# Start bytes of TensorE's operands in a decoder block: equal modulo 512 in output projection and MLP, eight other distances in the input projection

## The chip, the cores and the metric

One core of a Trainium2 chip runs the whole block in one launch. The metric is the device time in microseconds (us) of that launch; smaller is better.

## The reference

One decoder block on `x` of 2048 rows and 1024 columns, all in float32:

```python
h = rmsnorm(x, g_pre_mix)
proj = einsum('bsd,dc->bsc', h, w_in)             # 1024 x 3080
fox  = forgetting_attention(fq, fk, fv, f_logit)  # 8 heads of 64
diff = differential_attention(dq, dk, dv, ...)    # 4 heads of 2 x 64, values of 128
mix = einsum('bsc,cd->bsd', concatenate([fox, diff]), w_out)
x = x + rmsnorm(mix, g_post_mix)
h = rmsnorm(x, g_pre_mlp)
u = square(relu(einsum('bsd,df->bsf', h, w_up)))  # 1024 x 4096
x = x + rmsnorm(einsum('bsf,fd->bsd', u, w_down), g_post_mlp)
```

Both attentions are causal and take a softmax over the keys.

## The kernel before

The kernel keeps float32 accuracy by splitting each operand of a large product into a high and a low part (`_hi`, `_lo`) and running three matmuls for each: hi x hi, hi x lo and lo x hi. Nearly all of them are 128 x 128 stationary by 128 x 512 moving. In `nc.matmul(out, stationary, moving)` the second argument is loaded into the array by an instruction of its own (PEld in the profile) while the matmul before it is still streaming its moving operand; a profile's row names them the other way round, `out<-moving,stationary` (in the rows of L673 to L675 `pj_acc<-pj_v_hi,pj_h_early` has v_hi moving).

There are four stages, each with an order of work written out by hand for every engine.

- **Input projection** (`project`): the 16 tiles of normalised rows are turned and split into `keep.h_early` (rows 0 to 1023) and `h_late` (rows 1024 to 2047). For the q and k columns the weights `w_hi`, `w_lo` are stationary and h moves (L665 to L667); for the v columns h is stationary and `v_hi`, `v_lo` move (L673 to L675).
- **Attention** (`attend`): scores `ps_s` from `k1`, `k2` moving and `q1`, `q2` stationary (L1376, L1382), transposes of `probs` (L1400), and products with `v_sb` stationary and `p_hi`, `p_lo` moving (L1415 to L1420). A planner with costs and due times sets the order.
- **Output projection** (`mix_out`): for each of 16 tiles of rows `m_hi`, `m_lo` are stationary, `w_hi` and `w_lo` move (L1648 to L1650; for the last two of eight steps of k the low part is `keep.w_lo_end`, otherwise `w_lo_begin`), 48 matmuls, then 8 transposes (L1658) of the tile before.
- **MLP** (`mlp`): two halves of 1024 rows; in each, 16 chunks of 256 hidden columns. A chunk's first product (`up`, L2011 to L2014) has `up_hi`, `up_lo` stationary and `h2_rows_hi`, `h2_rows_lo` moving, 96 matmuls; its second product (`down`, L2032 to L2036) has `u_hi`, `u_lo` stationary and `dn_hi`, `dn_lo` moving, 96 matmuls in 16 groups of six, each added into `y` by VectorE (L1976). In the last chunk of a half VectorE normalises finished tiles (L1963) and GpSimd adds the residual (L1851).

All tiles in SBUF are taken from one pointer that runs upwards, through `Room.sb` (L41); each starts at the next multiple of 32 bytes. The rows of all these operands, and the steps between the slices that a matmul takes, are multiples of 512 bytes, so the start of a tile modulo 512 is the start of every slice of it. Worked out from the order of allocation:

| tiles | start, bytes modulo 512 | address range, bytes |
|---|---|---|
| `h_early`; `q1`, `q2`, `k1`, `k2`, `p_hi`, `p_lo`; `m_hi`, `m_lo`, `w_lo_end`; `u_hi`, `u_lo`; `ident_r` | 128 | below 98,944 |
| `h_late`, projection's `w_hi`, `w_lo`, `v_hi`, `v_lo` | 64 | 100,416 and up |
| `v_sb`, `probs`; `rows_hi`, `rows_lo`; output projection's `w_hi`, `w_lo_begin`; `up_hi`, `up_lo`, `dn_hi`, `dn_lo` | 320 | 99,648 and up |

Of the kernel before, what the change touches and what calls it, by code (L numbers as in the profile page):

```python
# [12 lines left out]
P = 128  # L13
# [16 lines left out]
def f32(ap):  # L30

    return ap.bitcast(F32)


class Room:
# [4 lines left out]

    def sb(self, name, shape, dt=F32):  # L41
        return self.ctx.enter_context(self.nc.sbuf_tensor(f"{self.stage}_{name}", shape, dt))

    def ps(self, name, shape):
        return self.ctx.enter_context(self.nc.psum_tensor(f"{self.stage}_{name}", shape, F32))
# [155 lines left out]
def project(nc, keep, x, g_pre_mix, w_in, b_forget, lams, g_subln, qk, vals, q_rows, k_rows):  # L201
# [36 lines left out]
    with ExitStack() as ctx:  # L238
        r = Room(nc, ctx, "pj")
# [3 lines left out]
        rstd = r.sb("rstd", [P, RT])  # L243
        power = r.sb("power", [P, 1])
        eps = r.sb("eps", [P, 1])
        h_late = r.sb("h_late", [P, 2, KT, S // 2], F32R)
        raw = r.sb("raw", [P, 2, KT, P])
        w_hi = r.sb("w_hi", [P, 2, KT, P], F32R)
        w_lo = r.sb("w_lo", [P, 2, KT, P], F32R)
        lam_in = r.sb("lam_in", [P, 4, HD])  # L250
        acc = r.ps("acc", [P, 8, 512])
        with ExitStack() as early:
            e_room = Room(nc, early, "pje")
            xin = e_room.sb("xin", [P, XR, D])
            xn = e_room.sb("xn", [P, 2, D])
            gain = e_room.sb("gain", [P, D])
            junk = e_room.sb("junk", [P, D], mybir.dt.bfloat16)
            wl_raw = e_room.sb("wl_raw", [P, KT, H])
            wl = e_room.sb("wl", [P, KT, 2 * H], F32R)
            b = e_room.sb("b", [P, 1])  # L260
            z, z2, az, e, w, lw, t1, c = (e_room.sb(name, [P, SEG])
                                          for name in ("z", "z2", "az", "e", "w", "lw", "t1", "c"))
            c_hi, c_lo = (e_room.sb(name, [P, SEG], F32R) for name in ("c_hi", "c_lo"))
            carry = e_room.sb("carry", [P, 1])
            ones, negs, zeros, tri = (e_room.sb(name, [P, SEG]) for name in ("ones", "negs", "zeros", "tri"))
            pos = e_room.sb("pos", [SEGS, SEG])
            up = e_room.sb("up", [SEGS, D4, SEG])
        v_hi = r.sb("v_hi", [P, KT, 512], F32R)
        v_lo = r.sb("v_lo", [P, KT, 512], F32R)

        x_loaded = [r.sem(f"x_loaded{s}") for s in range(XR)]
# [701 lines left out]
def attend(nc, keep, qk, vals, q_rows, k_rows, mixT, w_out, x):  # L973
# [44 lines left out]
    with ExitStack() as ctx:  # L1018
        r = Room(nc, ctx, "at")
        k1, k2, q1, q2, p_hi, p_lo = keep.k1, keep.k2, keep.q1, keep.q2, keep.p_hi, keep.p_lo  # L1020
        k_loaded, q_loaded = keep.k_loaded, keep.q_loaded
        ident_r, nlam, gsub = keep.ident_r, keep.nlam, keep.gsub
        ident = f32(ident_r[:, :])
        o_sb = r.sb("o_sb", [P, ORING, 512])
        v_sb = r.sb("v_sb", [P, 6, 4, 256], F32R)
        probs = r.sb("probs", [P, PROB_COLUMNS])
# [1016 lines left out]
def hybrid_block(nc, x, g_pre_mix, w_in, b_forget, lambda_q1, lambda_k1, lambda_q2, lambda_k2,  # L2043
                 g_subln, w_out, g_post_mix, g_pre_mlp, w_up, w_down, g_post_mlp, out):
    qk = nc.dram_tensor("qk", [16, 2, P, S], F32).ap()
    vals = nc.dram_tensor("vals", [2, 4, S, 256], F32).ap()
    q_rows = nc.dram_tensor("q_rows", [4, FOX_HEADS + DIFF_HEADS, S], F32).ap()
    k_rows = nc.dram_tensor("k_rows", [4, FOX_HEADS + DIFF_HEADS, S], F32).ap()
    mixT = nc.dram_tensor("mixT", [KT, P, S], F32).ap()
    x2 = nc.dram_tensor("x2", [S, D], F32).ap()  # L2050
    h2T = nc.dram_tensor("h2T", [2, KT, P, S // 2], F32).ap()
    with ExitStack() as ctx:
        keep = Lasting(nc, ctx)
        project(nc, keep, x, g_pre_mix, w_in, b_forget, (lambda_q1, lambda_k1, lambda_q2, lambda_k2), g_subln,
                qk, vals, q_rows, k_rows)
        attend(nc, keep, qk, vals, q_rows, k_rows, mixT, w_out, x)
        r = Room(nc, ctx, "h2")
        rows_hi = r.sb("rows_hi", [P, KT, S // 2], F32R)
        rows_lo = r.sb("rows_lo", [P, KT, S // 2], F32R)
        mix_out(nc, keep, mixT, x, g_post_mix, g_pre_mlp, x2, h2T, rows_hi, rows_lo, w_up)  # L2060
        mlp(nc, keep, rows_hi, rows_lo, h2T, w_up, w_down, x2, g_post_mlp, out)
# [22 lines left out]
```

How the kernel before makes its waits and increments, by code:

```python
    def wait_mixed(self, eng):  # L162
        for s in range(ORING):
            eng.wait_ge(self.o_stored[s], 16 * ((4 * 8 + ORING - 1 - s) // ORING))
# [170 lines left out]
        @block.sync  # L336
# [1 line left out]
            def load_x(t):  # L338
                if t >= XR:
                    sp.wait_ge(xn_ready, t - XR + 1)
                sp.dma_start(xin[:, t % XR, :], x[0, bass.ts(t, P), :]).then_inc(x_loaded[t % XR], 16)
# [1 line left out]
            def load_piece(z):  # L343
                what, n, _ = pieces[z]
                col = column_of(what, n)
                if z >= 2:
                    sp.wait_ge(w_ready, z - 1)
                sp.dma_start(raw[:, z % 2], w_v[:, :, col:col + P]).then_inc(raw_loaded[z % 2], 16)
# [6 lines left out]
            load_x(3)  # L355
            load_piece(0)
            load_x(4)
            load_piece(1)
            for t in range(5, RT):
                load_x(t)
            load_piece(2)
            load_piece(3)
            for job in jobs:
                if job.what == "logit":
                    sp.wait_ge(stored[job.out % OR], 16 * (job.out // OR + 1))
            for n, dst in enumerate((z, z2)):
                sp.dma_start(dst[:, :], logits[n].rearrange("h (s j) -> (h s) j", j=SEG)).then_inc(z_loaded, 16)
            for n, v in enumerate(lams):
# [4 lines left out]
            for job in jobs:  # L373
                if job.what == "qk" and job.n in (0, 4):
                    sp.wait_ge(stored[job.out % OR], 16 * (job.out // OR + 1))
            sp.wait_ge(rows_stored, ROWS)
```

## Time and profile before

| | us |
|---|---|
| median of 3 runs | 3103.01 |
| lowest and highest run | 3100.74, 3103.22 |
| the profiled execution | 3099.3 |
| its span, first to last instruction | 3096.9 |
| TensorE busy in it (matmuls) | 2952.1 |
| VectorE, ScalarE, GpSimd busy | 1678.8, 1022.6, 1005.6 |

The span falls into the projection (to about 583 us), attention (to 1424), the output projection (to 1636) and the MLP. A matmul's recorded duration runs on after the next one has started, so the sum of the durations of a line is not the time that it takes; the starts of consecutive matmuls give that. TensorE's clock has two levels, 1.2 and 2.4 GHz; in the profile's granted clock 1.00 is the higher.

### The profile page before, as it was taken

The page shows a single profiled execution, that of the slowest core. Times are in us where ns is not written, and L with a number is a line of the kernel's source. Part 1 is how long each engine was busy: PE and PEld are TensorE (multiplying, and loading weights), DVE is VectorE, ACT ScalarE, POOL GpSimd, SP SyncE. Part 2 cuts the span into 40 slices and gives each one's busy share as a digit, 9 for nine tenths or more (in the row PEclk, how much of TensorE's full clock was granted, in tenths as well). Part 3 has the DMA queues.
Part 4 walks back from the last instruction along what each step waited for, and adds up shares of the span by engine and source line. Part 5 has one row for each costly group of instructions (what it writes and reads, how often), then busy time and mean ns, then how long its engine had stood idle before and what let it go on. Part 6 is the DMA issues. An engine that isn't in the chain of part 4 may idle for free. (4 is left out here: it accounts for less than half of the span.)

```text
span 3096.9 us, 39329 instructions
## 1 busy us (share of the span) xinstructions
PE 2952.1 (95%) x14082; PEld 2411.1 (78%) x14082; DVE 1678.8 (54%) x2505; ACT 1022.6 (33%) x1973; POOL 1005.6 (32%) x733
## 2 busy tenths in 40 slices
PE   7999999998998989988998999999999999999996
PEld 5888888777877778877876888888887788888885
DVE  5211111389898898996554444444446544444446
ACT  4121111387786877863221111111112111111111
POOL 4220020157466465571113222222225222222224
PEclk9999999999999999999998999999999999999998
DMA  5342342833434144323732011101134110111022
GB/s 171 124 143 102 111 139 94 204 77 85 103 95 111 52 118 118 78 78 117 223 122 75 28 54 54 54 27 54 54 135 164 55 54 27 54 54 54 28 75 88
DMA packets 205240, 282.78 MB, mean 91 GB/s; under 512 B 12032, under 2 KB 135168, under 8 KB 205120
## 3 DMA queue, kind: packets, MB, share of 16 engines
q1 hardware_dynamic: 150976, 213.19, 23.7%
q10 hardware_dynamic: 53376, 67.25, 6.1%
q8 instruction: 70, 1.15, 0.2%
q0 software_dynamic: 768, 0.79, 0.1%
q14 instruction: 50, 0.41, 0.1%
HBM read 196.38 MB, written 84.80 MB: 91 GB/s over the span
## 5 line engine op out<-in xcount | busy, mean ns | idle before, releaser
L1976 DVE TENSOR_TENSOR ml_y<-ml_y,ml_ps_y 128x512 f32<-128x512 f32 x512 | 351.3, 686 | 246.9 <-PE ml_ps_y L2036 242.0
L2032 PE MATMUL ml_ps_y<-ml_dn_hi,ml_u_hi 128*128 128x512 f32 x1024 | 408.6, 399 | 10.5 <-DVE ml_y L1976 10.5
L2011 PE MATMUL ml_ps_u<-h_rows_hi,ml_up_hi 128*128 128x512 f32 x1024 | 400.7, 391 | 9.5 <-POOL ml_up_lo L1829 9.5
L2036 PE MATMUL ml_ps_y<-ml_dn_hi,ml_u_lo 128*128 128x512 f32 x1024 | 406.1, 397 | 0.0
L2034 PE MATMUL ml_ps_y<-ml_dn_lo,ml_u_hi 128*128 128x512 f32 x1024 | 406.1, 397 | 0.0
L2013 PE MATMUL ml_ps_u<-h_rows_lo,ml_up_hi 128*128 128x512 f32 x1024 | 400.3, 391 | 0.0
L2014 PE MATMUL ml_ps_u<-h_rows_hi,ml_up_lo 128*128 128x512 f32 x1024 | 400.1, 391 | 0.0
L1278 DVE TENSOR_REDUCE at_nmax<-at_ps_s 128x1 f32<-128x1024 f32 (+7 forms) x384 | 347.0, 907 | 47.8 <-PE at_ps_s L1382 43.4
L1952 DVE TENSOR_TENSOR ml_relu<-ml_relu 128x512 f32<-128x512 f32 x128 | 94.6, 739 | 492.0 <-ACT ml_relu L1915 492.0
L1836 POOL TENSOR_TENSOR ml_dn_lo<-ml_dn_raw,ml_dn_hi 128x1024 fp32r<-128x1024 f32 x64 | 155.6, 2454 | 546.1 <-ACT ml_dn_hi L1905 546.1
L1829 POOL TENSOR_TENSOR ml_up_lo<-ml_up_raw,ml_up_hi 128x1024 fp32r<-128x1024 f32 x64 | 168.4, 2653 | 500.0 <-ACT ml_up_hi L1895 500.0
L588 DVE SCALAR_TENSOR_TENSOR pj_out_sb<-pj_acc,pj_out_sb 128x512 fp32r<-128x512 f32 x96 | 66.4, 692 | 429.2 <-ACT pj_out_sb L524 429.2
L1287 DVE TENSOR_TENSOR at_p_lo<-at_ps_t,at_p_hi 128x512 fp32r<-128x512 f32 x480 | 280.4, 602 | 27.2 <-ACT at_p_hi L1249 25.5
L1400 PE MATMUL at_ps_t<-at_ident_r,at_probs 128*128 128x128 f32 x1632 | 250.9, 278 | 37.0 <-DVE at_p_lo L1287 32.4
L1249 ACT ACTIVATE at_p_hi<-at_ps_t 128x512 fp32r<-128x512 f32 x480 | 248.9, 532 | 92.9 <-PE at_ps_t L1400 59.2
L1905 ACT ACTIVATE ml_dn_hi<-ml_dn_raw 128x1024 fp32r<-128x1024 f32 x64 | 64.6, 1054 | 629.8 <-PE ml_ps_y L2036 606.7
L1240 ACT ACTIVATE at_probs<-at_ps_s,at_nmax 128x1024 f32<-128x1024 f32 (+7 forms) x256 | 237.6, 929 | 91.5 <-DVE at_nmax L1278 83.1
L1400 PEld LDWEIGHTS at_ps_t<-at_ident_r,at_probs 128*128 128x128 f32 x1632 | 196.5, 143 | 82.6 <-issue 33.5
L1915 ACT ACTIVATE ml_relu<-ml_ps_u 128x512 f32<-128x512 f32 x128 | 76.5, 599 | 554.2 <-PE ml_ps_u L2014 528.8
L2032 PEld LDWEIGHTS ml_ps_y<-ml_dn_hi,ml_u_hi 128*128 128x128 f32 x1024 | 193.1, 189 | 63.6 <-DVE ml_y L1976 18.5
L2011 PEld LDWEIGHTS ml_ps_u<-h_rows_hi,ml_up_hi 128*128 128x128 f32 x1024 | 193.4, 189 | 50.9 <-issue 10.3
L1376 PE MATMUL at_ps_s<-at_k,at_q 128*128 128x512 f32 (+3 forms) x640 | 213.8, 399 | 17.3 <-ACT at_probs L1240 14.2
(229 smaller groups left out, 5707.5 us busy)
## 6 DMA issues: line engine op xcount, KB each, us to landing
qk<-pj_out_sb ACTq DMA_DIRECT2D x64, 512.0 KB, 2.8
ml_up_raw<-in_w_up_dram SPq DMA_DIRECT2D x32, 1024.0 KB, 5.6
ml_dn_raw<-in_w_down_dram SPq DMA_DIRECT2D x32, 1024.0 KB, 7.6
at_q<-qk SPq DMA_DIRECT2D x96, 256.0 KB
at_k<-qk SPq DMA_DIRECT2D x96, 256.0 KB
vals<-pj_out_sb ACTq DMA_DIRECT2D x32, 512.0 KB, 2.9
at_v_sb<-vals SPq DMA_DIRECT2D x32, 512.0 KB, 3.9
pj_raw<-in_w_in_dram SPq DMA_DIRECT2D x24, 512.0 KB, 4.0
```

The source lines that it names most:

```text
L1240: act.activation(out, ps_s[:, sc.g % 2, 0:sc.width], ACT.Exp, bias=bias, accum_out=rsum[:, par, sc.a, s, sc.part:sc.part + 1]).then_inc(ex ...
L1249: act.activation(p_hi[:, t.n % PRING, t.off:512], ps_t[:, at % TRING, t.off:512], ACT.Copy)\
L1278: dve.tensor_reduce(nmax[:, par, sc.a, s, sc.part:sc.part + 1], ps_s[:, sc.g % 2, 0:sc.width], AX.X, ALU.max, negate=True).then_inc(maxed, 1)
L1287: dve.tensor_tensor(p_lo[:, t.n % PRING, t.off:512], ps_t[:, at % TRING, t.off:512], f32(p_hi[:, t.n % PRING, t.off:512]), ALU.subtract).t ...
L1400: last = pe.transpose(ps_t[:, at % TRING, a * P:(a + 1) * P], probs[:, key:key + P], ident)
L1976: dve.tensor_tensor(y[:, t, cols], y[:, t, cols], ps_y[:, b % 4, :], ALU.add)\
L2011: pe.matmul(ps_u[:, b % 4, :], up_hi[:, k, cols], h_hi[:, k, rows], start=(k == 0), stop=False)
L2013: pe.matmul(ps_u[:, b % 4, :], up_hi[:, k, cols], h_lo[:, k, rows], start=False, stop=False)
L2014: last = pe.matmul(ps_u[:, b % 4, :], up_lo[:, k, cols], h_hi[:, k, rows], start=False, stop=(k == KT - 1))
L2032: pe.matmul(ps_y[:, b % 4, :], u_hi[:, s, f, rows], dn_hi[:, f, cols], start=(f == 0), stop=False)
L2034: pe.matmul(ps_y[:, b % 4, :], u_hi[:, s, f, rows], dn_lo[:, f, cols], start=False, stop=False)
L2036: last = pe.matmul(ps_y[:, b % 4, :], u_lo[:, s, f, rows], dn_hi[:, f, cols], start=False, stop=(f == FT - 1))
```

## The change

A new method of `Room` places a tile without use, a gap, so that the next tile starts at a given byte modulo 512:

```diff
+    def start_at(self, offset):
+        base = -(-self.nc.sbuf_base // 32) * 32
+        if (offset - base) % 512:
+            self.sb(f"gap{base}", [P, (offset - base) % 512 // 4])
...
         eps = r.sb("eps", [P, 1])
+        r.start_at(96)
         h_late = r.sb("h_late", [P, 2, KT, S // 2], F32R)
         raw = r.sb("raw", [P, 2, KT, P])
+        r.start_at(128)
         w_hi = r.sb("w_hi", [P, 2, KT, P], F32R)
+        r.start_at(160)
         w_lo = r.sb("w_lo", [P, 2, KT, P], F32R)
...
+        r.start_at(224)
         v_hi = r.sb("v_hi", [P, KT, 512], F32R)
+        r.start_at(352)
         v_lo = r.sb("v_lo", [P, KT, 512], F32R)
...
         ident = f32(ident_r[:, :])
+        r.start_at(128)
         o_sb = r.sb("o_sb", [P, ORING, 512])
...
         r = Room(nc, ctx, "h2")
+        r.start_at(128)
         rows_hi = r.sb("rows_hi", [P, KT, S // 2], F32R)
```

No engine has an instruction more or less, or in another place; only addresses in SBUF change, and the line numbers (by 6 to 13). The tiles that follow a gap move with it:

| stage | tiles | before | after |
|---|---|---|---|
| projection | `h_early` | 128 | 128 |
| | `h_late` | 64 | 96 |
| | `w_hi`, `w_lo` | 64, 64 | 128, 160 |
| | `v_hi`, `v_lo` | 64, 64 | 224, 352 |
| attention | `v_sb`, `probs` | 320 | 128 |
| | `q1`, `q2`, `k1`, `k2`, `p_hi`, `p_lo` | 128 | 128 |
| output projection | `m_hi`, `m_lo`, `w_lo_end` | 128 | 128 |
| | `w_hi`, `w_lo_begin` | 320 | 128 |
| MLP | `rows_hi`, `rows_lo`, `up_hi`, `up_lo`, `dn_hi`, `dn_lo` | 320 | 128 |
| | `u_hi`, `u_lo` | 128 | 128 |

## Rows read from the trace of the kernel before

**Rows 1.** Stretches by stage: from:to, length, PE busy (count), PEld, DVE, ACT, POOL, clock

```profile
90.00:583.00 493.00, 493.00 (x2155) 404.24 (x2154) 66.45 (x108) 74.82 (x114) 62.02 (x28) 1.00 0.37 123
583.00:1424.00 841.00, 768.80 (x4548) 639.39 (x4546) 740.94 (x1340) 631.61 (x1428) 487.00 (x370) 0.98 0.39 97
1424.00:1636.00 212.00, 195.97 (x896) 159.35 (x896) 114.86 (x102) 58.13 (x88) 25.87 (x66) 0.96 0.53 159
1636.00:3097.00 1461.00, 1424.93 (x6144) 1157.05 (x6144) 709.16 (x914) 217.86 (x286) 387.31 (x190) 0.99 0.18 63
```

**Rows 2.** TensorE's waits over the span, longest: us in total, times, longest

```profile
PE at_ps_t L1400 <- DVE at_p_lo L1287: 32.4, 24, 5.6
```

**Rows 3.** TensorE in order of time, MLP: start us, us; first product, then second

```profile
1987.30 0.39 PE L2011 MATMUL ml_ps_u<-h_rows_hi,ml_up_hi 128*128 128x512 f32 x1
...
1995.24 0.39 PE L2014 MATMUL ml_ps_u<-h_rows_hi,ml_up_lo 128*128 128x512 f32 x1
...
2003.21 0.39 PE L2032 MATMUL ml_ps_y<-ml_dn_hi,ml_u_hi 128*128 128x512 f32 x1
...
2016.97 0.40 PE L2036 MATMUL ml_ps_y<-ml_dn_hi,ml_u_lo 128*128 128x512 f32 x1
```

**Rows 4.** Groups by line and shape, MLP: count, busy us, mean ns of one, idle

```profile
L2034 PE MATMUL ml_ps_y<-ml_dn_lo,ml_u_hi 128*128 128x512 f32 x1024 | 406.1, 397 | 0.0
...
L2013 PE MATMUL ml_ps_u<-h_rows_lo,ml_up_hi 128*128 128x512 f32 x1024 | 400.3, 391 | 0.0
```

**Rows 5.** The same view, projection

```profile
L665 PE MATMUL pj_acc<-pj_h_early,pj_w_hi 128*128 128x512 f32 x256 | 101.7, 397 | 0.0
L667 PE MATMUL pj_acc<-pj_h_early,pj_w_lo 128*128 128x512 f32 x256 | 100.5, 392 | 0.0
L665 PE MATMUL pj_acc<-pj_h_late,pj_w_hi 128*128 128x512 f32 x256 | 100.4, 392 | 0.0
L667 PE MATMUL pj_acc<-pj_h_late,pj_w_lo 128*128 128x512 f32 x256 | 99.9, 390 | 0.0
L666 PE MATMUL pj_acc<-pj_h_late,pj_w_hi 128*128 128x512 f32 x256 | 99.6, 389 | 0.0
L666 PE MATMUL pj_acc<-pj_h_early,pj_w_hi 128*128 128x512 f32 x256 | 99.6, 389 | 0.0
...
L673 PE MATMUL pj_acc<-pj_v_hi,pj_h_early 128*128 128x512 f32 x128 | 50.6, 396 | 0.0
...
L673 PE MATMUL pj_acc<-pj_v_hi,pj_h_late 128*128 128x512 f32 x128 | 49.8, 389 | 0.0
```

**Rows 6.** The same view, output projection: whole span, then 1466.13 to 1466.15 us

```profile
L1649 PE MATMUL mo_acc<-mo_w_lo_begin,mo_m_hi 128*128 128x512 f32 x180 | 71.1, 395 | 0.0
...
L1649 PE MATMUL mo_acc<-mo_w_lo_end,mo_m_hi 128*128 128x512 f32 x1 | 0.4, 388 | 0.0
```

**Rows 7.** The same view, attention: whole span, then 1109.00 to 1109.69 us

```profile
L1416 PE MATMUL at_ps_o<-at_p_lo,at_v_sb 128*128 128x512 f32 x224 | 88.2, 394 | 0.0
...
L1376 PE MATMUL at_ps_s<-at_k,at_q 128*128 128x512 f32 x2 | 0.6, 389 | 0.0
```

**Rows 8.** VectorE and TensorE in order of time, output projection: start us, us

```profile
1505.76 1.28 DVE L1591 SCALAR_TENSOR_TENSOR mo_xn<-mo_y,mo_rstd,mo_g_pre 128x1024 f32<-128x1024 f32 x1
...
1507.67 1.23 DVE L1578 TENSOR_TENSOR mo_m_lo<-mo_m_raw,mo_m_hi 128x1024 fp32r<-128x1024 f32 x1
...
1509.09 1.04 PE L1658 MATMUL mo_flip<-at_ident_r,mo_xn 128*128 128x128 f32 x8
1509.88 0.48 PE L1648 MATMUL mo_acc<-mo_w_hi,mo_m_hi 128*128 128x512 f32 x1
```

**Rows 9.** The chain that ended last, its end: start us, us, what

```profile
3061.87 0.24 PE ml_ps_y L2036
...
3064.17 2.41 POOL ml_xres L1851
...
3092.61 1.23 DVE ml_xres L1987
```

## The prediction

> **What bounds the kernel now.** Read the stretches first [rows 1]: TensorE is busy 493.0 of 493 us in the projection, 196 of 212 in the output projection and 1424.9 of 1461 in the MLP. Only attention leaves a real gap (768.8 of 841), and its longest wait in total is 32.4 us on VectorE [rows 2]. In three of four stages the time is therefore a count of matmuls times the distance from one start to the next. No instruction moves here, so the question is that distance, for matmuls with 512 columns.
>
> A matmul's recorded duration does not give it directly, since consecutive ones overlap. The starts do. In the MLP's first product 35 matmuls start between 1987.30 and 1995.24 us, 226.9 ns each; in its second product 59 start between 2003.21 and 2016.97, 233.2 ns each [rows 3]. (Starts are printed to 10 ns; I use 226.7 and 233.3.) The recorded durations over all 1024 of a line are 391 and 397 [rows 4]: about the spacing plus 162 to 164 ns, so differences between recorded means can be read as differences of spacing.
>
> Both products have the same shape, the same engine and the same weight load before each matmul. What differs in the table of bytes: in the first product the stationary tile (up_hi, up_lo) and the moving tile (rows_hi, rows_lo) both stand at 320 modulo 512; in the second the stationary tile (u) is at 128 and the moving one (dn) at 320. The projection has the same pair side by side. With the same v_hi and the same line, h_early (128 against 64) takes 396 and h_late (64 against 64) 389; with w_hi at 64, h_early's three lines take 397, 389 and 392, h_late's 392, 389 and 390 [rows 5]. So equal bytes give the cheap mark of 389, unlike ones mostly 392 to 397. While a matmul streams its moving operand, the next one's stationary operand is loaded (a PEld instruction beside each matmul), so I read this as the two reads meeting in SBUF, and the distance that counts as moving tile minus the stationary tile loaded meanwhile.
>
> **The change, part by part.**
>
> *MLP, second product.* All of u, dn_hi and dn_lo stand at 128, so distance 192 becomes 0. There are 32 passes of 96 matmuls. Thirty of them run on TensorE's path in full: 30 x 96 x 6.6 ns = 19.0 us. The last pass of each half hands over early: after its fifth group of six the chain goes to VectorE and then to GpSimd, which alone takes it from 3064 to the end at 3093 [rows 9]; only some 30 matmuls of each count, 0.4 us. Nothing takes the gain away: the next product waits for no other engine (TensorE busy throughout), and VectorE, which adds up every six matmuls, is busy 709 of 1461 us [rows 1]. Term: **-19.4 us**, bounds -18 (after a break a stream may need some matmuls until its spacing is regular) and -20.5.
>
> *MLP, first product.* From 320/320 to 128/128, distance 0 both times. Is 128 as good as 320? Two rows say yes: in the output projection w_lo_end (128) streams while m_lo (128) is loaded, and there the recorded time is 388 where w_lo_begin (320) has 395 over all [rows 6]; in attention a run of scores, keys and queries all at 128, shows 389 [rows 7]. Term: **0**.
>
> *Output projection.* m_hi, m_lo stay at 128, w_hi and w_lo_begin go from 320 to 128: distance 192 becomes 0. After each block of transposes the first matmul waits for its weights and keeps its time; 15 tiles x 47 x 6.6 ns = 4.7 us, less a little for settling. It must also reach the end: the normalised tile is ready at 1507.04 for transposes at 1509.09, and the split of the next input at 1508.90 for a product at 1509.88 [rows 8]. Slack 2.0 and 1.0 us, and the period shrinks by 0.3. Term: **-4.2 us**, bounds -3.5 and -4.7.
>
> *Attention.* v and probs move to 128, so the products with v go from distance -192 to 0; scores were at 0. At most 784 full-width matmuls (two lines of 224, three of 112) x (394 - 389) = 3.9 us [rows 7]. But scores already have equal bytes and their runs are two to six matmuls between transposes, too short to settle. And this stage waits on other engines too. Term: **-0.5 us**, bounds -3.9 and +0.5 (no row shows equal bytes slower than unlike ones, so the loss is bounded by that alone).
>
> *Projection.* Here bytes that agree are pulled apart. Distances (moving minus stationary): h_early/w_hi 0 (was 64), h_early/w_lo -32 (64), h_late/w_hi -32 (0), h_late/w_lo -64 (0), v_hi/h_early 96 (-64), v_hi/h_late 128 (0), v_lo/h_early 224 (-64), v_lo/h_late 256 (0). Before, the spacing sums to 768 x 231.0 + 768 x 228.5 + 384 x 233.2 + 384 x 226.8 ns = 529.5 us (each mean is the busy time of its lines in [rows 5] over their count, less 162 ns; the two v groups by one line of three). Of the new distances the trace shows 0 (226.7) and, for v, -64 (233.3). Bounds from rows: all at 226.7 gives 522.3 us, -7.2; all at the 397 of h_early's dearest line, 235, gives +11.9. I take 233.3 for every distance but 0, the value that both 192 and -64 have and hence the nearest: h_late with w 768 x 233.3 (+3.7), v with h_late 384 x 233.3 (+2.5), v with h_early unchanged (0), and h_early with w, where two of three loads are at 0, 228.9 (-1.6). Term: **+4.7 us**. TensorE is busy without a break, so all of it counts.
>
> **Sum.** -19.4 - 4.2 - 0.5 + 4.7 = -19.4 us. The profiled execution took 3099.3 us (span 3096.9 and 2.4 around it), so 3079.9 for it; the runs' median is 3103.0, 3.7 higher, so **3083.6**. With the bounds of MLP, output projection and attention, and the projection between 0 and +8.1 (all at 233.3): 3077 to 3092.
>
> **The rivals.**
>
> *The projection's new distances are cheap.* If all are near 226.7, its term is -7 and the time 3072 (3068 to 3077). For: distance 64 is not uniformly dear, one of h_early's lines has 389. Against: -64, one of the new distances, is in the trace and dear.
>
> *They are dearer than anything seen.* At 235 the term is 12 and the time 3091; with starts at odd multiples of 32 (96, 160, 224, 352), which no operand of these matmuls has now, up to 3097. Nothing shows such a step; nothing excludes it.
>
> *It doesn't do what it says: the tile's place matters, not its byte.* Before the change all tiles at 128 lie below address 98,944 and all at 64 or 320 above it, so "both tiles in the same part of the memory" sorts every row as well as "both at the same byte": u and dn, h_early and v_hi, m and w_lo_begin are pairs across that border and dear, h_late and w, rows and up above it, w_lo_end and m_lo below it cheap [rows 3 to 6]. By place, moving tiles up by 32 to 320 bytes changes nothing: 3103. Against it: two reads that get in each other's way should do so within one part, not across two.
> The Trainium skill's rule would also end here: "TensorE: Matmul & The Clock Gate", Step-by-step: what each phase is for, says that TensorE has two independent SBUF read ports and that loading the next weights takes no bandwidth from the running matmul; by it no start byte could change the spacing, and the sum would be 0. The trace does not agree that the spacing is free of where the operands lie: 396 against 389 with one line and one v_hi [rows 5].
>
> *Slower: what is fast is the byte 64 modulo 256, not equality.* Every long cheap stretch now has both operands at 64 or 320, every dear one an operand at 128. Then MLP and output projection, all at 128, are dear: the second product gains nothing and the first loses 32 x 96 x 6.6 ns = 20.3 us; with +4.7 in the projection 3128. It decides in the first product: slower as soon as its recorded mean rises from 391 by over 5 ns with none gained in the second. Against it stand the 388 and 389 at 128 [rows 6, 7], short stretches both.
>
> **How the numbers follow.** Forecast 0.63, cheap projection 0.15, dear projection 0.09, nothing changes 0.09, slower 0.04. The likeliest case gives 3083.6. The range 3070 to 3094 takes the forecast, most of the cheap case and half of the dear one: 0.8. A measurement of this kernel can tell about 0.2% from no change, 6.2 us, so faster means below 3096.8: 0.63 + 0.15 + 0.08 = 0.86; same 0.10 (place, and what is left of the dear case); slower 0.04.
>
> **What would show it.** Right: L2013 and L2034 of before, by their new line numbers, both at a recorded 389 to 392; the output projection's lines at 389 to 391 apart from the first after transposes; h_late's lines near 395, v's near 395. The forecast falls if the MLP's first product leaves 391, or if the second stays at 397. If both hold and the time is off, the projection's rows say by how much each distance differs from 233.3.

## Result and profile after

The changed kernel takes 3087.44 us (median of 4 runs, 3082.47 to 3087.71); the kernel before, run beside it, 3101.88 us. The ratio is 0.9949, with a 95% interval of 0.9935 to 0.9964: 14.4 us faster. The profiled execution of the changed kernel took 3087.21 us, its span 3085.1.

First the stretches by stage (columns as in [rows 1]; each stretch begins and ends at about the first matmul of a stage):

```profile
90.00:592.00 502.00, 499.76 (x2159) 404.43 (x2157) 67.17 (x109) 75.44 (x115) 61.93 (x28) 1.00 0.37 122
592.00:1431.00 839.00, 769.32 (x4544) 640.62 (x4544) 740.89 (x1340) 631.69 (x1428) 487.68 (x370) 0.97 0.39 97
1431.00:1638.00 207.00, 191.84 (x896) 159.58 (x896) 114.26 (x101) 57.52 (x87) 25.55 (x66) 0.96 0.54 162
1638.00:3085.00 1447.00, 1408.08 (x6144) 1156.47 (x6144) 707.74 (x914) 217.71 (x286) 382.83 (x190) 0.99 0.18 63
```

Taken from the first matmul of each stage to the first of the next, in the two profiled executions:

| stage | before, us | after, us | difference | predicted |
|---|---|---|---|---|
| projection | 577.7 | 583.7 | +6.05 | +4.7 |
| attention | 838.6 | 839.0 | +0.3 | -0.5 |
| output projection | 211.4 | 207.3 | -4.1 | -4.2 |
| MLP, to the end | 1460.8 | 1446.7 | -14.1 | -19.4 |
| sum | | | -11.9 | -19.4 |

(By the spans the kernels are 11.9 us apart, by the medians 14.4: the profiled execution of before lay 3.7 us under the median that the prediction started from, that of after 0.2 us under its own.)

The groups by line and shape, whole span: count, busy us, mean ns of one, idle time before them and what ended it. The first lines are the MLP's (L2046 and L2025 answer to L2034 and L2013 in [rows 4]), then the projection's (L676 to L678 are L665 to L667 of [rows 5], L684 and L686 are L673 and L675), the output projection's (L1661 is L1649 of [rows 6]) and one of attention (L1428 is L1416 of [rows 7]):

```profile
L2044 PE MATMUL ml_ps_y<-ml_dn_hi,ml_u_hi 128*128 128x512 f32 x1024 | 404.1, 395 | 14.4 <-DVE ml_y L1988 14.4
L2046 PE MATMUL ml_ps_y<-ml_dn_lo,ml_u_hi 128*128 128x512 f32 x1024 | 400.5, 391 | 0.0
L2025 PE MATMUL ml_ps_u<-h_rows_lo,ml_up_hi 128*128 128x512 f32 x1024 | 399.4, 390 | 0.0
...
L677 PE MATMUL pj_acc<-pj_h_early,pj_w_hi 128*128 128x512 f32 x256 | 102.1, 399 | 0.0
L676 PE MATMUL pj_acc<-pj_h_early,pj_w_hi 128*128 128x512 f32 x256 | 101.7, 397 | 0.0
L677 PE MATMUL pj_acc<-pj_h_late,pj_w_hi 128*128 128x512 f32 x256 | 101.0, 394 | 0.0
L678 PE MATMUL pj_acc<-pj_h_late,pj_w_lo 128*128 128x512 f32 x256 | 100.4, 392 | 0.0
L678 PE MATMUL pj_acc<-pj_h_early,pj_w_lo 128*128 128x512 f32 x256 | 99.7, 389 | 0.0
...
L1428 PE MATMUL at_ps_o<-at_p_lo,at_v_sb 128*128 128x512 f32 x224 | 88.4, 394 | 0.0
L1661 PE MATMUL mo_acc<-mo_w_lo_begin,mo_m_hi 128*128 128x512 f32 x180 | 70.1, 389 | 0.0
...
L684 PE MATMUL pj_acc<-pj_v_hi,pj_h_early 128*128 128x512 f32 x128 | 50.8, 397 | 0.0
...
L684 PE MATMUL pj_acc<-pj_v_hi,pj_h_late 128*128 128x512 f32 x128 | 50.0, 391 | 0.0
L686 PE MATMUL pj_acc<-pj_v_lo,pj_h_late 128*128 128x512 f32 x128 | 49.7, 388 | 0.0
```

The reader is to see three things. The second product's L2034, at 397 before, is L2046 at 391 now, and the output projection's 395 is 389: where bytes became equal, the matmuls became cheap. In the projection both of h_early's lines with w_hi stand at 397 and 399 although their own two tiles start at the same byte. And v_lo with h_late, 256 apart, is at 388, as cheap as anything here.

The 391 of L2046 is what was predicted, the time of the stage is not. The starts say why. TensorE in order of time in a second product (start us, us), around its 24th matmul, the last of its fourth group of six:

```profile
2000.25 0.39 PE L2044 MATMUL ml_ps_y<-ml_dn_hi,ml_u_hi 128*128 128x512 f32 x1
2000.48 0.39 PE L2046 MATMUL ml_ps_y<-ml_dn_lo,ml_u_hi 128*128 128x512 f32 x1
2000.71 0.39 PE L2048 MATMUL ml_ps_y<-ml_dn_hi,ml_u_lo 128*128 128x512 f32 x1
2001.02 0.50 PE L2044 MATMUL ml_ps_y<-ml_dn_hi,ml_u_hi 128*128 128x512 f32 x1
2001.36 0.39 PE L2046 MATMUL ml_ps_y<-ml_dn_lo,ml_u_hi 128*128 128x512 f32 x1
2001.59 0.40 PE L2048 MATMUL ml_ps_y<-ml_dn_hi,ml_u_lo 128*128 128x512 f32 x1
```

The matmul at 2001.02 comes 317 ns after the one before it, the next 338 ns later, and the six after that are 231, 236, 228, 233, 231 and 226 ns apart before the rhythm of 226, 227, 227 is back. (Starts stand in the trace to the nanosecond; spacings below are from those.) That is the first matmul of the fifth group of six; it seems to wait for a bank of ps_y, a buffer of TensorE's results, that VectorE has not yet added into y (the run with the wait, below, tests this). VectorE and GpSimd in order of time, the same place (start us, us; x5 are five instructions in a row; the last column is idle time before and what ended it):

```profile
1997.14 0.43 DVE L1967 CAST ml_u_hi<-ml_relu 128x512 fp32r<-128x512 f32 x1
1997.61 2.77 DVE L1969 TENSOR_TENSOR ml_u_lo<-ml_relu,ml_u_hi 128x512 fp32r<-128x512 f32 x1
2000.30 3.56 DVE L1988 TENSOR_TENSOR ml_y<-ml_y,ml_ps_y 128x512 f32<-128x512 f32 x5
...
1997.41 5.22 POOL L1841 TENSOR_TENSOR ml_up_lo<-ml_up_raw,ml_up_hi 128x1024 fp32r<-128x1024 f32 x2 [17.52 <-ACT ml_up_hi L1907]
```

VectorE's first add starts at 2000.30, five follow back to back because their groups were already done, and the subtraction ahead of them, u_lo, took 2.77 us while GpSimd was at its own subtraction of the next weights. In the kernel before the same instruction takes as long and the same bank is late, but its matmuls were slower and reached that bank later: there the two spacings are 230 and 307 ns.

### The profile page after: what moved, and what is told of

It is laid out like the page before. It is cut to its first block and busy times, and to the rows that moved or that the text cites. A ratio compares the mean times of both kernels' runs of the same rounds, so it can differ in the third digit from the quotient of the medians.

```text
span 3085.1 us, 39329 instructions
## 1 busy us (share of the span) xinstructions
PE 2938.5 (95%) x14082; PEld 2411.9 (78%) x14082; DVE 1677.5 (54%) x2505; ACT 1022.6 (33%) x1973; POOL 1001.3 (32%) x733
## 5 line engine op out<-in xcount | busy, mean ns | idle before, releaser
L2044 PE MATMUL ml_ps_y<-ml_dn_hi,ml_u_hi 128*128 128x512 f32 x1024 | 404.1, 395 | 14.4 <-DVE ml_y L1988 14.4
L2046 PE MATMUL ml_ps_y<-ml_dn_lo,ml_u_hi 128*128 128x512 f32 x1024 | 400.5, 391 | 0.0
L2025 PE MATMUL ml_ps_u<-h_rows_lo,ml_up_hi 128*128 128x512 f32 x1024 | 399.4, 390 | 0.0
L1412 PE MATMUL at_ps_t<-at_ident_r,at_probs 128*128 128x128 f32 x1632 | 251.1, 278 | 36.8 <-DVE at_p_lo L1299 31.9
```

Source lines behind the costliest of these rows:

```text
L1412: last = pe.transpose(ps_t[:, at % TRING, a * P:(a + 1) * P], probs[:, key:key + P], ident)
L2025: pe.matmul(ps_u[:, b % 4, :], up_hi[:, k, cols], h_lo[:, k, rows], start=False, stop=False)
L2044: pe.matmul(ps_y[:, b % 4, :], u_hi[:, s, f, rows], dn_hi[:, f, cols], start=(f == 0), stop=False)
L2046: pe.matmul(ps_y[:, b % 4, :], u_hi[:, s, f, rows], dn_lo[:, f, cols], start=False, stop=False)
```

## Experiments

The theory when the experiments began: the distance of the two start bytes sets the spacing of matmuls with 512 columns, distances that are multiples of 512, perhaps of 256, give 226.7 ns; the missing part of the MLP's gain is VectorE's late add. Rivals: another mechanism in the projection (a price of the place, or of each tile's own byte), another loss in the MLP (the second half's start, the end).

### Every operand at the same byte

```diff
-        r.start_at(96)    # h_late
+        r.start_at(128)
-        r.start_at(160)   # w_lo
+        r.start_at(128)
-        r.start_at(224)   # v_hi
+        r.start_at(128)
-        r.start_at(352)   # v_lo
+        r.start_at(128)
```

> The changed kernel with the projection's tiles also at 128, so that every matmul's moving tile and the stationary tile loaded meanwhile start at the same byte modulo 512. Theory 1 (the distance sets the spacing): all 512-column lines of the projection at a recorded 389 to 390, its 2304 matmuls at 226.7 ns, so the projection about 13 us shorter than after the change and 7 shorter than before; time about 3074 us, ratio to before 0.991. Theory 2 (the starts at odd multiples of 32, and not the distance, make the projection dear after the change): the projection only returns to its time of before, 6 us shorter than after the change; about 3081 us, 0.9935.

Measured: 3072.75 us, 0.9913 [0.9897, 0.993] of the kernel before (the brackets hold the 95% interval, here and below). The projection takes 572.5 us, against 577.7 before and 583.7 with the change: 5.2 and 11.2 us less, where 7 and 13 were expected. Its dearest and cheapest lines (groups by line, whole span):

```profile
L676 PE MATMUL pj_acc<-pj_h_early,pj_w_hi 128*128 128x512 f32 x256 | 100.5, 392 | 0.0
...
L677 PE MATMUL pj_acc<-pj_h_early,pj_w_hi 128*128 128x512 f32 x256 | 99.6, 389 | 0.0
...
L684 PE MATMUL pj_acc<-pj_v_hi,pj_h_late 128*128 128x512 f32 x128 | 49.8, 389 | 0.0
```

The unequal bytes of the projection are thus worth 11.2 us (583.7 less 572.5), and the 397 and 399 of h_early's lines are not a property of h_early.

### The two halves of the change apart

The change of the projection alone (the five start_at lines of `project`), and that of the MLP alone (the one line in the stage h2, on the kernel before).

> Only the projection's starts of the change (96, 128, 160, 224, 352), all else as before. Both theories: projection about 6 us longer than before, from its first matmul to the first of attention 583.7 against 577.7 us, nothing else moved; about 3108 us, ratio 1.002.

Measured: 3106.95 us, 1.0022 [1.0012, 1.0031]. The projection grows by 6.1 us, as in the full change.

> Only the start of the h2 tiles (output projection and MLP at 128), projection and attention as before. If the parts add up: output projection 4 us and MLP 14 us shorter than before, about 3084 us, ratio 0.994. If what the MLP gained had depended on where attention's tiles lie, less.

Measured: 3077.66 us, 0.992 [0.9903, 0.9936]. That is lower than the 3084 expected. From the first matmul of the MLP to the end it takes 1447.0 us, as in the changed kernel (1446.7). The output projection fell as well, to 207.1 us from 211.4, though its own line was not there: w_hi and w_lo_begin lie behind rows_hi and rows_lo, and the one gap moved them too. The two parts add up: by the medians +7.4 and -21.9 us against the kernel before beside them (3099.53), together -14.5, where the whole change gave -14.4; by the spans 3106.4 + 3078.8 - 3096.9 = 3088.3, against 3085.1. So no dependence of one half on the other shows, within what executions of one kernel differ by (3097 to 3104 for the kernel before).

### A map of the distances

A kernel with nothing but streams of 72 matmuls, each stream with its own start bytes for the stationary tile `wt` and the moving tile `mv`. One stream of it, with mv 8 float32, that is 32 bytes, above wt (broken into three lines here; the other streams have other numbers in place of 0 and 8):

```diff
+            for k in range(N): last = pe.matmul(acc[:, 1, :],
+                wt[:, 0 + k % 6 * 128:0 + k % 6 * 128 + 128],
+                mv[:, 8 + k % 4 * 512:520 + k % 4 * 512], start=k == 0, stop=k == N - 1)
```

> Nothing of the block is computed: 25 streams of 72 matmuls with 512 columns run one after another on copies of x, each at one distance (moving minus stationary start, modulo 512), 16 distances in steps of 32 with the stationary tile at 0, then distance 0 with both tiles at 32, 64 and 192, distances 64 and -64 with the stationary tile at 32 and 64, and four streams with only 16 stationary columns. Theory 1: spacing 226.7 ns at distance 0 wherever both tiles start, 229 to 240 at the others, and the same value for a distance at either place; with 16 stationary columns less of it, since fewer bytes are loaded. Theory 2: streams with both tiles at 32 are dear at distance 0 too, and the even multiples of 64 are cheap.

Six of the 25 streams (groups by line; L165 both tiles at byte 32, L133 distance -256, L109 64, L117 128, L125 192, L185 distance 0 with 16 stationary columns):

```profile
L125 PE MATMUL map_acc<-map_mv,map_wt 128*128 128x512 f32 x72 | 17.1, 397 | 0.7 <-ACT map_res L94 0.7
...
L117 PE MATMUL map_acc<-map_mv,map_wt 128*128 128x512 f32 x72 | 17.1, 396 | 0.7 <-ACT map_res L94 0.7
...
L185 PE MATMUL map_acc<-map_mv,map_wt 128*16 128x512 f32 x72 | 16.8, 394 | 0.7 <-ACT map_res L94 0.7
L109 PE MATMUL map_acc<-map_mv,map_wt 128*128 128x512 f32 x72 | 16.8, 393 | 0.7 <-ACT map_res L94 0.7
...
L133 PE MATMUL map_acc<-map_mv,map_wt 128*128 128x512 f32 x72 | 16.6, 391 | 0.7 <-ACT map_res L94 0.7
L165 PE MATMUL map_acc<-map_mv,map_wt 128*128 128x512 f32 x72 | 16.6, 391 | 0.7 <-ACT map_res L94 0.7
```

And the settled spacing, the mean over the later starts of each stream, by moving minus stationary byte:

| distance | spacing, ns |
|---|---|
| 0 (both at 0, 32, 64 or 192) and -256 | 226.67 |
| 64 and -192 | 228.9 |
| 32, 96, 128, 192, 224; -224, -160, -128, -64, -32 | 233.3 to 233.4 |
| 160, -96 | 234.2, 234.3 |
| 0, 64, 192, -64 with 16 stationary columns | 231.1, 231.7, 231.7, 231.7 |

So the period is 256 bytes, not 512, among these steps of 32: -256 is as good as 0, and -192 equals 64, -96 equals 160. Equal bytes are cheap wherever they are (0, 32, 64, 192). In the 16 first streams the stationary tile stays at 0, so that the distance is also the moving tile's own byte; two more streams tell them apart: distance 64 with the stationary tile at 32 gives 228.9 again, -64 with it at 64 gives 233.3 again. The expectation that a load of 16 columns makes matmuls cheaper fell: their spacing is 231.1 ns even at distance 0. The load itself is shorter (PEld rows of the same run: 95 ns recorded, against 188 with 128 columns), and the distance then makes only 0.6 ns.

### Patterns, fine distances, other shapes

A second kernel of that kind, with 23 streams.

> Computes nothing of the block: 23 streams of 72 matmuls, each into one bank, spacing of the starts to be read per stream. (1) Which two tiles count: matmuls whose own operands lie at equal bytes while the moving operand and the stationary operand loaded meanwhile lie 128 apart, and the reverse. Theory 1 (the running matmul's moving operand meets the next one's stationary load): 233.4 ns for the first, 226.7 for the second. Rival (own pair counts): 226.7 and 233.4. (2) Copies of three patterns of the projection after the change. Theory 1 with a settled value that builds up over many equal matmuls: loads at 0, -32, 0 about 233 ns each (as in the changed kernel: 228, 233, 239), where a price per matmul would give 228.9; loads at -32, -64, -32 about 231; loads at 128, 128, 256 about 229, where 233.4 would follow if 256 were unlike. (3) Distances of 4, 8, 16, -16 and -4 bytes: if only an exact multiple of 256 is cheap, 229 to 234 ns each; if the unit is 32 or 64 bytes, 4 to 16 give 226.7. (4) 64 and 32 stationary columns: 226.7 at distance 0 if the price comes with the amount loaded, 231 as with 16 columns if a short load is dear by itself. (5) 384 and 256 moving columns: at distance 128 some 4 to 7 ns over distance 0 as with 512 columns, or nothing. (6) bf16 operands at 0, 32, 64, 128, 192: half the bytes per row; theory 1 expects a difference between 0 and 128, smaller than 6.7 ns; the rival that it comes from float32 alone expects none.

Five of its lines (L119 loads at 0, -32, 0 as h_early with w after the change, L139 distance 16, L143 distance -16, L183 and L191 bf16 at 32 and 128; of the bf16 streams one or two records are missing):

```profile
L119 PE MATMUL map_acc<-map_mv,map_wt 128*128 128x512 f32 x72 | 17.1, 396 | 0.5 <-ACT map_res L100 0.5
...
L139 PE MATMUL map_acc<-map_mv,map_wt 128*128 128x512 f32 x72 | 16.9, 396 | 0.5 <-ACT map_res L100 0.5
...
L143 PE MATMUL map_acc<-map_mv,map_wt 128*128 128x512 f32 x72 | 16.6, 391 | 0.5 <-ACT map_res L100 0.5
L183 PE MATMUL map_acc<-map_mvb,map_wtb 128*128 128x512 bf16 x71 | 15.7, 379 | 0.6 <-ACT map_res L100 0.5
L191 PE MATMUL map_acc<-map_mvb,map_wtb 128*128 128x512 bf16 x71 | 15.7, 379 | 0.6 <-ACT map_res L100 0.5
```

| stream | settled spacing, ns |
|---|---|
| loads at 0, -32, 0 | 233.33 (228, 233, 239 in turn) |
| loads at -32, -64, -32 | 231.1 |
| loads at 128, 128, 256 | 228.9 |
| own pair 0, pair that meets 128 / own 128, meets 0 | 228.3 / 230.0 |
| distance 4, 8, 16, -4 | 236.7, 233.3, 231.7, 232.3 |
| distance -16 | 226.67 |
| 64 columns stationary, distance 0 / 128; 32 columns, 0 | 230.0 / 229.3; 231.7 |
| 384 columns moving, 0 / 128 | 173.3 / 176.0 |
| 256 columns moving, 0 / 128 | 120.0 / 118.6 |
| bf16, any distance | 215.8 |

The first three copy the projection after the change, and agree with it: in h_early with w the starts of the changed kernel run 228, 233, 239 too. With one unlike load in three the mean of the three is as dear as that of a stream with unlike loads alone. That refutes a price per matmul. Which two tiles count is not settled by the fourth line: with the assumption of the prediction (the moving tile against the stationary tile loaded meanwhile) it should have been 233.4 and 226.7, with the matmul's own two tiles 226.7 and 233.4, and it is neither. With bf16 the bytes don't matter at all, and with 256 moving columns equal ones are even slightly dearer.

### 256 apart

The change's own bytes, with the other partner 256 away instead of at the same byte.

```diff
-        r.start_at(96)    # h_late; the six other start_at lines likewise
+        r.start_at(384)
```

> The bytes of the changed kernel with another choice: h_late, w_hi, w_lo, v_hi, v_lo, v_sb, probs and the MLP's rows, up and dn at 384 modulo 512, and h_early, the queries and keys, p, m and u at 128 as before, so that every pair is either equal or 256 apart. Theory from the streams measured alone (the period is 256): all lines of projection and MLP at a recorded 389 to 392, time as with everything at 128, 3073 (3070 to 3077), 0.991. Rival (the period in the kernel is 512 as the change's own words have it, 256 as dear as 192 or 64): h_early with w, v with h_early and the MLP's second product at 397 or 396, time 3095 to 3103, 0.998 to 1.000.

Measured: 3075.05 us, 0.9919 [0.9903, 0.9936]: what the kernel with everything at 128 gives (0.9913), not 3095 to 3103. One line of each disputed kind, with h_early against v_lo and u against dn now 256 apart:

```profile
L2046 PE MATMUL ml_ps_y<-ml_dn_lo,ml_u_hi 128*128 128x512 f32 x1024 | 399.2, 390 | 0.0
...
L678 PE MATMUL pj_acc<-pj_h_early,pj_w_lo 128*128 128x512 f32 x256 | 99.7, 389 | 0.0
...
L686 PE MATMUL pj_acc<-pj_v_lo,pj_h_early 128*128 128x512 f32 x128 | 49.8, 389 | 0.0
```

The pairs 256 apart are as cheap in the kernel as in the map.

### VectorE's late add

The kernel with everything at 128, and GpSimd made to wait until VectorE has done the last u_lo of a pass:

```diff
                     if not isinstance(c, int) or w == 0:
+                        pool.wait_ge(u_step, 6 + 3 * UB * (n + 2))
                         lo_up(n + 2)
```

> All operands at byte 128 as in the run with everything equal, and one wait more: in the MLP's second product GpSimd begins to split the next weights (up_lo) only after VectorE has finished the last u_lo of the pass. Theory (VectorE's u_lo of 2.8 us, lengthened by GpSimd's work beside it, delays its first add into y, and with it TensorE's fifth group of each pass): u_lo falls to 1 us or less, the spacing of 317 and 338 ns in the middle of a second product goes back to under 250, a pass of 96 matmuls from 21.99 to about 21.77 us, the kernel from 3072.8 to about 3066.5 us, 0.989 of the kernel before. Rival (the add is late for another reason, such as ScalarE's relu or the order on VectorE's queue): u_lo or the stall stays as it was and the time is 3073 within 2 us. Slower, 3080 and up, if GpSimd's weights then come too late for the next first product.

Measured: 3060.07 us (3057.06 to 3062.27), 0.9869 [0.9853, 0.9886]: 12.7 us less than without the wait, where 6 were expected. VectorE and GpSimd in order of time, and TensorE's groups by line:

```profile
1979.92 0.43 DVE L1968 CAST ml_u_hi<-ml_relu 128x512 fp32r<-128x512 f32 x1
1980.38 0.69 DVE L1970 TENSOR_TENSOR ml_u_lo<-ml_relu,ml_u_hi 128x512 fp32r<-128x512 f32 x1
1980.99 1.40 DVE L1989 TENSOR_TENSOR ml_y<-ml_y,ml_ps_y 128x512 f32<-128x512 f32 x2
...
1981.24 4.76 POOL L1841 TENSOR_TENSOR ml_up_lo<-ml_up_raw,ml_up_hi 128x1024 fp32r<-128x1024 f32 x2 [18.58 <-DVE ml_u_lo L1970]
```

```profile
L2045 PE MATMUL ml_ps_y<-ml_dn_hi,ml_u_hi 128*128 128x512 f32 x1024 | 398.7, 389 | 8.1 <-DVE ml_y L1989 8.1
L2049 PE MATMUL ml_ps_y<-ml_dn_hi,ml_u_lo 128*128 128x512 f32 x1024 | 398.6, 389 | 0.0
L2047 PE MATMUL ml_ps_y<-ml_dn_lo,ml_u_hi 128*128 128x512 f32 x1024 | 398.5, 389 | 0.0
```

u_lo takes 0.69 us instead of 2.77, two adds stand in a row instead of five, and GpSimd's own pair of instructions is shorter too, 4.76 instead of 5.22. Every regular second product takes 21.76 us, just what 96 x 226.7 ns gives, without the two long spacings. The kernel gained more than expected at two places that the expectation left out: the first second product of the first half falls from 24.75 us to 21.76, and the passage between the halves by 4.4 us. Not all of the latter is the wait's: over the passage TensorE's granted clock is 0.96 without the wait and 0.99 with it, and the next section has a kernel with the wait and 0.96. The Trainium skill has the rule behind it ("SBUF — State Buffer", Who interferes with whom): a VectorE instruction with two inputs in SBUF contends with a GpSimd instruction that reads SBUF, and whoever issues first keeps the other out. The trace of the changed kernel agrees: GpSimd's first subtraction ran from 1997.41 to 1999.82, u_lo from 1997.61 to 2000.37, four times its 0.69 us, so that it ended 0.55 us after GpSimd's.

### The same wait in the kernel before and in the changed one

> The kernel before with the one wait of the run with the wait added: GpSimd begins to split the next chunk's up_lo only after VectorE's last u_lo of the pass. Theory (the contention between the two cost the kernel before little, since its slower matmuls hid it, and the changed kernel more): a second product falls from 22.47 us only to 96 x 233.3 ns = 22.40, so 28 regular passes give 2 us; with the first pass of each half (27.3 us now, 22.4 without a stall) and a little at the handover some 8 to 12 us: MLP 1449 to 1453 us, kernel 3089 to 3093, 0.997. Rival (the wait is worth as much in the kernel before as beside equal bytes, 13.7 us, because it speeds something else up): 3087, MLP 1447.

Measured: 3087.95 us, 0.9965 [0.9952, 0.9977]; regular second products 22.40 us, as 96 x 233.3 ns. The time lies 1 us under the theory's range and 1 us over the rival's figure; the MLP, 1449.2 us, and the second products are as the theory had them.

> The changed kernel with that same wait. Against the kernel before with the wait, the change alone is left, with no stall of VectorE in either. Theory: the MLP then gives what was predicted for it, 30 x 96 x 6.67 = 19.2 us (18 to 20.5): MLP 1430, kernel about 3074.5, 0.991 of the kernel before. Rival (something other than the stall took 5 us of the MLP's gain): the difference between the two kernels' MLP stays at 14 us.

Measured: 3071.87 us, 0.9909 [0.9892, 0.9925]; regular second products 21.76 us. The MLP's stretch in the two (columns as in [rows 1]), the kernel before with the wait:

```profile
1635.00:3084.00 1449.00, 1418.39 (x6144) 1156.06 (x6144) 643.47 (x914) 217.78 (x286) 374.05 (x189) 0.99 0.18 63
```

and the changed kernel with it:

```profile
1639.00:3071.60 1432.60, 1401.93 (x6144) 1158.56 (x6144) 642.80 (x914) 217.79 (x286) 369.52 (x190) 0.99 0.18 64
```

From the first matmul of the stage to the end they take 1449.2 and 1432.2 us: the change is worth 16.9 us there, against 14.1 without the wait and 18 to 20.5 expected; between the kernel before with the wait and the one with everything at 128 and the wait (1430.1) it is 19.1. VectorE's busy time in the stretch is 643 us, against 709.16 in [rows 1]: 66 us less, 57 of them in u_lo (94.9 against 151.9 us). The theory holds for the regular passes in full (0.64 us each, predicted 0.634).

What is left, 2.1 us in one of these pairs and nothing in the other, lies in the passage between the halves, from the last two second products of the first half to the first of the second. It takes 118.5 to 125.6 us in the nine profiled kernels of the block; 120.7 in the changed kernel with the wait and 118.5 with everything at 128 and the wait, whose bytes in the MLP are the same. TensorE's clock differs there. In both kernels TensorE waits for VectorE's add in the second half's first second product; the 5.94 us behind that wait are, in the changed kernel (columns as in [rows 1])

```profile
2395.88:2401.82 5.94, 5.94 (x14) 4.68 (x15) 3.05 (x5) 0.00 (x0) 4.23 (x2) 0.50 0.06 15
```

and with everything at 128

```profile
2384.96:2390.90 5.94, 5.94 (x26) 4.92 (x27) 4.16 (x7) 0.00 (x0) 4.27 (x2) 1.00 0.06 12
```

At a granted clock of 0.50, the level of 1.2 GHz, 14 matmuls fit in, 427 ns apart, at 1.00 there are 26. Twelve matmuls fewer are 2.7 us at 227 ns; TensorE's wait ahead of them was 0.6 us shorter in the changed kernel (2.85 us against 3.47), which leaves the 2.1. The clock was low behind the shorter wait and high behind the longer one, so the length of that wait alone does not decide it. Over the whole passage the granted clock is 0.96 in the kernel before, the changed one, the one with everything at 128 and the changed one with the wait, 0.99 in the two others with the wait. So the 4.4 us that the passage lost in the section above are in part the clock's; in the changed kernel, at 0.96 both times, the wait took 3.2 us off it (123.9 to 120.7).

The kernel with everything at 128 and the wait, 3060.07 us, beats both the kernel before and the changed one.

## Why the prediction was right or wrong

The direction was right and the time inside the range, 3087.4 against 3083.6. By its own steps:

- **How spacing is read.** Recorded mean less 162 to 164 ns, and 226.7 against 233.3 ns: both as read for streams without a break. The map gives 226.67 at distance 0 and 233.3 at 192. The mean of a line also holds the first matmuls behind a break, which equal bytes don't shorten (nine of the 256 of L665 with h_early are recorded at over 420 ns), so the projection had 5.2 us to give with all bytes equal, not the 7.2 of the prediction's bound.
- **MLP, first product, 0.** Right: 390 after, 391 before; its passes went from 21.78 to 21.76 us, 0.6 us over all. One of the two rows behind it did not carry it, though: the 388 of [rows 6] is one matmul out of 60, and the line as a whole stood at 393, nearly as dear as the 395 beside it:

```profile
L1649 PE MATMUL mo_acc<-mo_w_lo_end,mo_m_hi 128*128 128x512 f32 x60 | 23.6, 393 | 0.0
```

  So here the forecast was better than its evidence. With the 390 the rival of byte 64 modulo 256 is out, and so is the rival of the place: u and dn still lie on either side of the border and are cheap now. The Trainium skill's "TensorE: Matmul & The Clock Gate" (Step-by-step: what each phase is for) has two independent read ports and a weight load that takes nothing from the running matmul; the map does not agree for float32 with 512 columns (226.7 against 233.3 ns by start byte alone); for bf16 it shows no such difference (215.8 at each of five distances).
- **MLP, second product, -19.4.** The mechanism was right, the size was not: -14.1. The step that failed is the sentence that nothing takes the gain away because VectorE is busy only 709 of 1461 us. That is a mean over the stage. In the first 5 us of each pass VectorE is late, and a faster TensorE only arrives earlier at the same bank. 26 regular passes went from 22.47 to 21.99 us, 0.48 each instead of 0.634: 0.13 us of the difference is the bank (317 + 338 ns instead of 230 + 307), the rest the six matmuls that settle again. That is 4.0 us of the 5.3 missing. The rest lies where the halves meet (-0.2, where the sum had counted -1.5: two full passes and the 0.2 of a last one) and at the stage's start, where TensorE runs at the lower clock for 4.9 us (1638.41 to 1643.35, granted 0.50) and before for 3.7 (1636.15 to 1639.90, granted 0.51). The runs with the wait show it: without the late add a pass gains 0.64 us.
- **Output projection, -4.2.** Right, -4.1. The settling after each block of transposes is in the spacings (after a first one of 313: 229, 233, 236, 224, 231, 236, 228, 233, 231, 226 ns in about half of the blocks; after 314: 232, 231 and then 227 in the others), and the slacks of [rows 8] were enough.
- **Attention, -0.5.** +0.3, and not to be told from nothing: kernels with the same tiles there take 837.3 to 840.5 us. Its lines are as before (L1428 at 394), which fits runs too short to settle, and so is its longest wait (TensorE's waits: us in total, times, longest), 31.9 us where [rows 2] has 32.4:

```profile
PE at_ps_t L1412 <- DVE at_p_lo L1299: 31.9, 22, 5.6
```

- **Projection, +4.7.** +6.05, with two of four parts far off. h_late with w +2.8 (predicted +3.7) and v with h_early 0.0 (0) were near. h_early with w was +2.4 instead of -1.6: the step that failed is the mean of two loads at 226.7 and one at 233.3. v with h_late was +0.8 instead of +2.5: 256 was counted as unlike, and is like. The two misses, +4.0 and -1.7, partly cancel, which is luck. The choice of 233.3 for every new distance was right to 0.1 ns in streams of one distance, except for 256 (226.67); for mixed ones it was not.
- **The rivals on the projection.** Not cheap (the term would be -7) and not dear (+12). The odd multiples of 32 cost 233 to 234 ns, no more than most even ones.
- **The range.** The bounds of the parts as stated, added up, give 3074 to 3090 us and not 3077 to 3092; 3087.4 lies in both.

## What to carry to other kernels

Where TensorE streams float32 matmuls of 512 columns without a break, put the stationary and the moving tiles at the same byte modulo 256, all that follow one another in a stream: it cost nothing here and gave 14 us in the MLP and 5 in the projection, against the kernel before. Before a gain per instruction is multiplied by the count, look at one pass in order of time for the first bank that another engine has to free: a busy share of a half says nothing about the first microseconds of a pass. A subtraction of two SBUF tiles on VectorE beside one on GpSimd can cost four times its time, and one wait that orders the two came with an MLP shorter by 11.6 us (kernel before), 13.7 (everything at 128) and 14.4 (changed kernel) here, a part of it by TensorE's clock.

## What was not expected of the hardware

- The period of the start byte is 256 in steps of 32, and distance -16 is as cheap as 0 (226.67 ns) while 16, 8, 4 and -4 cost 231.7 to 236.7 (each in one stream, for the negative ones with the moving tile at 0).
- The price belongs to a rhythm, not to a matmul: equal bytes 226, 227, 227; distance 192 236, 231; loads at 0, -32, 0 in turn 228, 233, 239. After a break it takes six matmuls (second product) and three or ten (after transposes) to return.
- A smaller weight load does not bring the matmuls closer together: at equal bytes 128 columns give 226.7 ns, 64 give 230.0, 32 give 231.7 and 16 give 231.1, though the load's own recorded time falls from 188 ns to 134, 109 and 95. With 64 and 16 columns the distance makes less than 1 ns.
- With bf16 operands, 215.8 ns at every distance; with 256 moving columns, 120.0 at distance 0 and 118.6 at 128: the effect is gone or turned round.
- Why -16 is cheap, and which two of the tiles meet, stays open.
